# Gates and output product of the second layer multiplied as high and low parts, with high parts made by GpSimd

## The reference, cut to what matters

```
proj = h @ o_w_in                                   # h: 256 x 1024
(q_c, kc_, vc_, ks_, vs_, kw_, vw_, g_c, z_c, q_d, k_d, v_d, z_d) = split(proj)
o_c = nsa_attention(...)       # compressed, selected and window keys, 8 heads of 64
y_c = merge_heads(o_c) * silu(z_c)                  # 256 x 512
o_d = banded_attention(...)    # window 128, with sinks
y_d = merge_heads(o_d) * silu(z_d)                  # 256 x 512
y   = concatenate([y_c, y_d])                       # 256 x 1024
x   = x + y @ w_out[1]
```

## Time and profile before

| | |
|---|---|
| median of 3 runs | 909.28 us (907.03 to 910.65) |
| profiled execution | 910.96 us |
| its span | 909.2 us |
| mean granted clock of TensorE | 0.994 |
| busy: PE, PEld, DVE, ACT, POOL | 882.9, 826.0, 428.8, 446.7, 609.0 us |
| L656, GpSimd's subtractions, largest group | 328 times, mean 1313 ns |
| L1374, ScalarE's high parts | 82 times, mean 1914 ns |

### The profile page before, as it was taken

The page is one execution under the profiler, slowest core; times in us unless marked ns, Lnnn a source line. Parts: engine busy times, 40 slices in busy tenths (PEclk is TensorE's granted clock), DMA queues, the critical chain, the costliest instruction groups (busy, mean ns, idle before and its releaser), DMA issues.

```text
span 909.2 us, 16515 instructions
## 1 busy us (share of the span) xinstructions
PE 882.9 (97%) x6792; PEld 826.0 (91%) x6792; DVE 428.8 (47%) x952; ACT 446.7 (49%) x665; POOL 609.0 (67%) x485
## 2 busy tenths in 40 slices
PE   6999999899999999999999999999999999999997
PEld 5898889897777999888988799999999999999996
DVE  3998665743875466882445232331124562211001
ACT  3434667344555453354444547586334775533330
POOL 0766468740000669989777777768889999997880
PEclk9999999999999999999999999999999999999999
DMA  9844577783210279597666444444536655545421
GB/s 347 344 146 158 214 243 266 252 307 131 100 48 1 93 275 391 219 376 261 226 213 232 149 176 145 154 167 156 216 139 232 231 185 187 185 141 186 185 94 47
DMA packets 27907, 177.61 MB, mean 195 GB/s; under 512 B 3080, under 2 KB 5780, under 8 KB 7480
## 3 DMA queue, kind: packets, MB, share of 16 engines
q1 hardware_dynamic: 26248, 174.35, 53.1%
q10 hardware_dynamic: 1584, 2.20, 0.7%
HBM read 174.95 MB, written 3.43 MB: 196 GB/s over the span
## 4 chain that ended last, share of the span: by engine, by line
PE 90%; DVE 4%; ACT 2%; issue 1%; DMA 1%; POOL 1%; ACTq 0%; DVEq 0%; SPq 0%
PE proj L742 18%; PE proj L744 18%; PE proj L745 18%; PE proj L717 5%; PE proj L822 3%; PE proj L819 3%; PE proj L821 3%; PE proj L1016 3%; PE proj L778 2%; PE mixed L968 1%; PE proj L1089 1%; PE transposed L937 1%; PE scores L923 1%; PE mixed L951 1%; PE sums L876 1%
## 5 line engine op out<-in xcount | busy, mean ns | idle before, releaser
L656 POOL TENSOR_TENSOR w_lo<-raw,w_hi 128x512 fp32r<-128x512 f32 x328 | 418.9, 1313 | 208.2 <-ACT w_hi L1374 208.1
L744 PE MATMUL proj<-parts,w_lo 128*128 128x256 f32 x952 | 266.4, 280 | 0.6 <-POOL w_lo L656 0.6
L742 PE MATMUL proj<-parts,w_hi 128*128 128x256 f32 x904 | 257.3, 285 | 0.5 <-POOL w_lo L656 0.3
L745 PE MATMUL proj<-parts,w_hi 128*128 128x256 f32 x904 | 252.6, 279 | 0.0
L1374 ACT ACTIVATE w_hi<-raw 128x2048 fp32r<-128x2048 f32 x82 | 156.8, 1914 | 112.4 <-DMA raw<-in_weights 61.0
L744 PEld LDWEIGHTS proj<-parts,w_lo 128*128 128x128 f32 x952 | 179.1, 188 | 1.7 <-POOL w_lo L656 0.8
L742 PEld LDWEIGHTS proj<-parts,w_hi 128*128 128x128 f32 x904 | 169.9, 188 | 2.8 <-issue 2.1
L745 PEld LDWEIGHTS proj<-parts,w_hi 128*128 128x128 f32 x904 | 170.4, 188 | 0.0
L656 POOL TENSOR_TENSOR w_lo<-arena,w_hi 128x512 fp32r<-128x512 f32 (+2 forms) x44 | 56.2, 1317 | 56.5 <-ACT w_hi L1374 56.5
L742 PE MATMUL proj<-hid_hi,w_hi 128*128 128x256 f32 x160 | 45.3, 283 | 0.0
L819 PE MATMUL proj<-w_hi,parts 128*128 128x512 f32 x112 | 45.0, 402 | 0.0
(11 more groups left out here) (402 smaller groups left out, 2111.7 us busy)
## 6 DMA issues: line engine op xcount, KB each, us to landing
raw<-in_weights SPq DMA_DIRECT2D x105, 1024.0 KB, 5.0
arena<-in_weights SPq DMA_DIRECT2D x32, 1024.0 KB, 7.2
wide<-in_weights SPq DMA_DIRECT2D x9, 1024.0 KB, 7.0
probT<-in_weights SPq DMA_DIRECT2D x8, 1024.0 KB, 5.6
dil_lines<-dil_line SPq DMA_DIRECT2D x1, 2304.0 KB, 12.9
prob<-in_weights SPq DMA_DIRECT2D x2, 1024.0 KB, 4.9
dil_bias<-dil_lines SPq DMA_DIRECT2D x1, 1536.0 KB, 9.4
xT<-in_x SPq DMA_DIRECT2D x2, 512.0 KB, 5.8
```

The costliest lines, as they stand in the source:

```text
L656: nc.gpsimd.tensor_tensor(lo_slots[RAW_AT[n]][:, at], raw_slots[RAW_AT[n]][:, at], hi_slots[HI_AT[m]][:, at].bitcast(F32), ALU.subtract).t ...
L742: nc.tensor.matmul(dst, whi, h, start=first, stop=False)
L744: nc.tensor.matmul(dst, wlo, h, start=False, stop=False)
L745: last = nc.tensor.matmul(dst, whi, lo[:, k, :], start=False, stop=stop)
```

## The change

Seven units more are split: zc1, zd0, zd1, wo1_0 to wo1_3. For the last six (`PLACED`) GpSimd makes the high part itself, four copies of 128x512 (`high`), ahead of the four subtractions; ScalarE skips them in `passing`. The operand of the output product, y, is split in four pieces of two row blocks (`gathered_high` on ScalarE, `parts_low` on VectorE, new entries `L:y0`, `L:y1` of the table), and the first products of wo1_0 and wo1_1 are made side by side, on piece 0 in one round and on piece 1 in the next. The loads of ak2_0, ak2_1 and rq0 stand in the natural order, and from wo1_0 to ak2_1 a fourth slot for high parts is used, `w_hi_b`, over the space of `dil_bias`. The high parts of ak2_0, ak2_1 and rq0 are made at passing wo1_1, wo1_2 and wo1_3, one each.

```diff
 FILL_CD = [x.split() for x in (
-    "N:kd E:zc0", "zc1.0 E:kd", "zc1.1", "E:zc1", "modA zd0.0.0", "zd0.0.1 E:modA", "", "zd0.1", "zd1.0 E:zd0", "", "zd1.1.0",
-    "zd1.1.1", "", "H:wo1_0 E:zd1", "H:wo1_1", "")]
+    "N:kd E:zc0", "zc1.0 E:kd", "zc1.1", "E:zc1", "modA zd0.0.0", "zd0.0.1 E:modA", "",
+    "zd0.1", "zd1.0 E:zd0", "", "zd1.1.0", "zd1.1.1", "L:y0", "H:0 E:zd1 L:y1", "H:1", "")]
+PLACED = ("zd0", "zd1", *(f"wo1_{i}" for i in range(4)))
...
-SPLIT_SOON = ["bq1", "bk0", "bk1", "bv0", "bv1", "zb0", "zb1", "za0", "za1"] + [f"wo0_{i}" for i in range(4)] + ["kcvc", "kskw", "vsvw", "qc0", "qc1", "vdgt", "qd0", "qd1", "kd"]
+SPLIT_SOON = ["bq1", "bk0", "bk1", "bv0", "bv1", "zb0", "zb1", "za0", "za1"] + [f"wo0_{i}" for i in range(4)] + ["kcvc", "kskw", "vsvw", "qc0", "qc1", "vdgt", "qd0", "qd1", "kd", "zc1", *PLACED]
...
-    return EARLY if n >= WEIGHT_AT["wo1_0"] else [*range(NRAW), *EARLY]
+    return [*range(NRAW), *EARLY]
 
 
 RAW_AT, RAW_BEFORE = take_slots(WEIGHTS, raw_slots_of)
-HI_AT, HI_BEFORE = take_slots(SPLIT, lambda n, u: range(NHI + sum(n >= SPLIT_AT[start] for start in HI_MORE)))
+SHARED_HI = SPLIT[SPLIT_AT["wo1_0"]:SPLIT_AT["ak2_1"] + 1]
+HI_AT, HI_BEFORE = take_slots(SPLIT, lambda n, u: [*range(NHI), NHI + 1] if u in SHARED_HI else range(NHI + sum(n >= SPLIT_AT[start] for start in HI_MORE)))
...
-for _us, _before in ((BEFORE_NORM["x2"], "wo1_2"), (("rq0",), "wo1_3"), *(((u,), before) for u, before in zip(ADA_FIRST, FIRST_BEFORE)), *(((u,), before) for u, before in zip(ADA_LATE, LATE_BEFORE)),
+for _us, _before in (*(((u,), before) for u, before in zip(ADA_FIRST, FIRST_BEFORE)), *(((u,), before) for u, before in zip(ADA_LATE, LATE_BEFORE)),
...
+            def quarters(u):
+
+                kt, w = unit_shape(u)
+                return [slice(kt * w // 4 * i, kt * w // 4 * (i + 1)) for i in range(4)]
+
+            def high(u):
+
+                n, m = WEIGHT_AT[u], SPLIT_AT[u]
+                pool.wait_ge(proj_ready, GROUP_AT["zc0"] + 1 if u == SHARED_HI[0] else LAST_READ[SPLIT[HI_BEFORE[m]]] + 1)
+                pool.wait_ge(raw_in[RAW_AT[n]], raw_target(n))
+                for at in quarters(u):
+                    nc.gpsimd.tensor_copy(hi_slots[HI_AT[m]][:, at], raw_slots[RAW_AT[n]][:, at]).then_inc(sem("hi_pool"), 1)
+
             def low(u):
 
                 n, m = WEIGHT_AT[u], SPLIT_AT[u]
-                kt, w = unit_shape(u)
-                pool.wait_ge(hi_ready, m + 1)
-                for i in range(4):
-                    at = slice(kt * w // 4 * i, kt * w // 4 * (i + 1))
+                if u not in PLACED:
+                    pool.wait_ge(hi_ready, m + 1 - sum(SPLIT_AT[v] < m for v in PLACED))
+                for i, at in enumerate(quarters(u)):
+                    if u in PLACED:
+                        pool.wait_ge(sem("hi_pool"), 4 * PLACED.index(u) + i + 1)
                     nc.gpsimd.tensor_tensor(lo_slots[RAW_AT[n]][:, at], raw_slots[RAW_AT[n]][:, at],
                                             hi_slots[HI_AT[m]][:, at].bitcast(F32), ALU.subtract).then_inc(lo_ready, 1)
 
...
-                if u == "ak2_0":
+                if u == "zc1":
                     pool.wait_ge(proj_ready, GROUP_AT["hidv"] + 1)
                     nc.gpsimd.memset(probT[:, 0:512], 0.0).then_inc(sem("cmp_zero"), 1)
+                if u in PLACED:
+                    high(u)
                 low(u)
...
                 elif name[:2] == "H:":
-                    output_half(name[2:], 0, yT1, y_of)
+                    n = int(name[2:])
+                    state["pair"] = two_units(("wo1_0", "wo1_1"), gathered(n, n + 1), state["pair"] if n else None, done=False)
...
-            def output_half(name, half, y, piece):
-
-                plain(name, y, piece, range(KD // 2 * half, KD // 2 * (half + 1)), fresh=half == 0, done=half == 1)
+            def gathered(lo, hi):
+
+                return [((2 * n, 2 * n + 1), every, lambda k, n=n: pe.wait_ge(y_ready, 4 + n + 1)) for n in range(lo, hi)]
...
-                if i < 2:
-                    output_half(f"wo1_{i}", 1, yT1, y_of)
-                else:
-                    plain(f"wo1_{i}", yT1)
+                if i == 0:
+                    two_units(("wo1_0", "wo1_1"), gathered(2, 4), state["pair"])
+                elif i > 1:
+                    project(f"wo1_{i}")
...
-            def passing(name, most=len(SPLIT)):
-
...
+                    if v in PLACED:
+                        state["hi"] += 1
+                        continue
...
-                    nc.scalar.activation(dst, ready(name)[:], ACT.Tanh, scale=0.5).then_inc(sem("z_tanh"), 1)
+                    nc.scalar.activation(dst, ready(name, name not in PLACED)[:], ACT.Tanh, scale=0.5).then_inc(sem("z_tanh"), 1)
+                elif name[:3] == "L:y":
+                    gathered_high(int(name[3:]))
...
+            def gathered_high(n):
+
+                operand_high([(hi_of(n), two(yT1, n), [(proj_ready, GROUP_AT["zd1"] + 1), (po_free, STEPS_TO["b"] + 2 * n + 2)])])
...
             narrow_attention(PART["c"] + PART["d"], FILL_CD)
+            for n in (2, 3):
+                gathered_high(n)
             table(ACT.Sqrt)
             output_parts(1, "x2", gain1, 0)
...
+                elif name[:3] == "L:y":
+                    parts_low(yT1, [int(name[3:])])
...
-            narrow_attention(PART["c"] + PART["d"], FILL_CD, 1)
+            narrow_attention(PART["c"] + PART["d"], FILL_CD, 1, lambda: parts_low(yT1, [2]))
+            parts_low(yT1, [3])
```

More of the change, by code:

```diff
@@ L1171, in around_norm @@
                 gained_products(name, 1, range(KD))
-            y_of = lambda k: pe.wait_ge(po_free, STEPS_TO["b"] + 2 * (k // 2) + 2) if k % 2 == 0 else None
             def convolved_product(i):
@@ L1326, in _ @@
                 if name[1] == "r":
-                    wait = (lambda k: pe.wait_ge(y_ready, 4 + k // 2 + 1)) if i == 0 else None
+                    wait = (lambda k: pe.wait_ge(y_ready, 8 + k // 2 + 1)) if i == 0 else None
                     features(name, None, yret_lo, [[(f"{name}{x}", 0, 0)] for x in "ab"], wait)
@@ L1333, in merged_product @@
                 if i == 0:
-                    ready = lambda k: pe.wait_ge(y_ready, 12 + k // 2 + 1)
+                    ready = lambda k: pe.wait_ge(y_ready, 16 + k // 2 + 1)
                     two_units(("wo2_0", "wo2_1"), [(range(6), every, ready), (range(6, KD), every, ready)])
@@ L1356, in _, with passing @@
             state = dict(hi=0)
-            def passing(name, most=len(SPLIT)):
-                while state["hi"] < min(len(SPLIT), most):
+            def passing(name):
+                while state["hi"] < len(SPLIT):
                     m = state["hi"]
@@ L1368, in passing @@
                     kt, w = unit_shape(v)
-                    if HI_BEFORE[m] is not None:
-                        act.wait_ge(proj_ready, LAST_READ[SPLIT[HI_BEFORE[m]]] + 1)
-                    elif v in HI_MORE:
+                    if v in HI_MORE:
                         act.wait_ge(po_free, STEPS_TO["a"])
+                    elif old >= 0:
+                        act.wait_ge(proj_ready, old + 1)
                     act.wait_ge(raw_in[RAW_AT[n]], raw_target(n))
```

## The result

The changed kernel takes 917.9 us (median of 5 runs, 917.75 to 920.61) against 909.67 us (median of 5, 907.03 to 910.65): a ratio of 1.0108, 95% interval 1.009 to 1.0127, so it is slower by 8.2 us. Its profiled execution is one of 917.87 us with a span of 916.1, 6.9 us over both numbers of before.

A forecast was written before the change was run, and what follows sets the result against it. Bound: the VectorE–TensorE loop over the second layer's attention units, little slack on either. Terms −2.9 + 2.4 + 8.9 − 3.8 + 1.0 = +5.6 us on 910.96 gave 916.6, less 1.7 for the median: 914.9 us, range 905 to 921.

The forecast's parts named there:

- the step from profiled execution to median: Whole kernel: the median of the runs lies 1.7 us below the profiled execution, taking 916.6 to 914.9 us.
- shorter filling, what comes through: 64 split products inside the second layer's attention stage: −6.0 us in all, of which −2.9 us comes through.
- detour of y: Attention rounds: VectorE waits for ScalarE's high part of y's piece 0, making unit 13's transposes +2.4 us later.
- held time, with the clock: Attention stage: GpSimd's pieces hold VectorE's operations with two SBUF inputs, +8.9 us, plus lower TensorE clock, +1.0 us.
- end of the output product: 48 output products after the last mixing, split: 16.8 us for 20.64, −3.8 us.
- my walk: The sixteen attention rounds stepped through with the rows' durations: 16 holds, together 10.5 us, +8.9 us after slack.
- The clock: Attention stage: TensorE's clock falls after waits, 1.67 us for one fall; +1.0 us over before, bounds −1.7 and +6.7.
- The signs: Trace afterwards: L1943 at 1.9 to 2.3 us beside GpSimd, transposes of rounds 1 to 4 waiting 1 to 1.5 each.
- Only half of the hold: Attention stage: GpSimd's copies leave VectorE alone, only subtractions hold it; +2.2 us, 911.5 us; chance 0.28.
- Faster: Attention stage: holds fall in VectorE's slack or small operations slip between pieces; 903.3 to 905.0 us; chance 0.15.

The follow-up runs named there:

- no_gpsimd_y_behind: no_gpsimd_work with y's two subtractions inside the rounds put behind the normalising of units 13 and 14 on VectorE; 904.24 us.
- no_gpsimd_work: Changed kernel with GpSimd's copies and subtractions for the seven units cut to 128x2 copies, TensorE taking those weights from the operand's high part; 906.98 us.
- gates_only: Kernel before with only zc1, zd0 and zd1 split, GpSimd making the high parts of zd0 and zd1, output product plain; 910.23 us.
- half_pieces: Changed kernel with GpSimd's copies and subtractions of the six units cut into 128x256 pieces, twice as many of half the length; 925.89 us.
- y_one_round_later: Changed kernel with L:y0, L:y1 and the first products of wo1_0 and wo1_1 one round later; 920.17 us.
- y_later_with_gap: y_one_round_later with GpSimd's work on wo1_0 begun only after TensorE's sp_kd group, giving GpSimd a pause between two units; 917.87 us.
- output_only: Changed kernel with only wo1_0 to wo1_3 split, zc1, zd0, zd1 plain, high parts in the three usual slots; 924.83 us.
- late_units_early_loads: Kernel before with only wo1_2 and wo1_3 split, GpSimd starting on them after the last normalising, loads and slots rearranged so nothing is late; 907.54 us.

## Why the prediction was right

The direction and the mechanism were right, and the size nearly, in part by luck: +5.6 us forecast on the profiled execution, +6.9 measured (+8.2 between the medians, for my profile of before was 1.3 us above its median of five). The forecast of 914.9 was 3.0 us short of 917.9: 1.3 are the sum's, and 1.7 come from the step from profiled execution to median, which the changed kernel doesn't have (917.87 and 917.9).

| term | forecast | measured | from |
|---|---|---|---|
| shorter filling, what comes through | −2.9 | −1.5 | no_gpsimd_y_behind, stage 67.7 − 69.2 |
| detour of y | +2.4 | +1.7 | stage 69.4 − 67.7 |
| held time, with the clock | +8.9 + 1.0 | +9.8 | stage 79.2 − 69.4 |
| end of the output product | −3.8 | −3.5 | 17.1 − 20.6 |

The measured terms make +6.5 of the 6.9. They are differences taken one after another, on kernels without GpSimd's work first; in another order the overlaps would be shared out differently.

- *Held time.* 16 holds and 10.5 us were forecast, 16 holds and 9.07 us are in the trace. The copies are shorter than taken: 2.29/4 = 0.57 us for 0.7. That is also below the 0.77 us that the Trainium skill gives for 512 elements (page "GPSIMD Engine Reference", section 3.1, on elementwise cycle accounting), so here the measurement decides. By my walk shorter copies had to make the stage shorter than the +8.4 forecast; it came out at +10.0. The same page's rule of section 8, that GpSimd contends with VectorE where this has two SBUF inputs or runs in its 2-port mode, doesn't disagree with the trace: L1943 is held, and L1901, with an input in PSUM, isn't (1.11 us at 282.77 for four over 128x128, beside GpSimd). L1915, of one input, is held too; whether it ran in the 2-port mode the trace doesn't show.
- *The clock* was mis-sized. It was half in 227 to 233, 254 to 257 and 271 to 274. The last two falls follow waits on L1943 (1.09 us ahead of 253.37, 2.27 ahead of 269.74); the first began before the wait of 2.41 us, behind one of 0.90. Against the same work at the full clock it cost 0.45 (transposes at 230.50), 1.1 (the split products behind, 4.04 for 2.98), 1.67 (mixing at 253.96) and 1.0 (mixing at 270.8, 2.5 for 1.5), 4.2 us for 1.67 before: +2.5 or more where +1.0 stood. That and 9.1 of holds make 11.6, and 1.8 of it was under cover. As the two together are 9.8 us, some 7.3 are left for the holds where 8.9 stood. That the pair comes to 9.8 for a forecast 9.9 is luck: one was too large by about what the other was too small.
- *The filling* gave half of what I let through, and the detour 0.7 less than charged; these two errors cancel in part. In the changed kernel the wait of VectorE on ScalarE is short (0.68 us ahead of L2073), since VectorE was late anyway, but the subtraction stands in front all the same: L1928, whose exponentials were ready, starts 1.7 us after the end of L1920, with the normalising and TensorE's wait of 2.87 us behind it. So the detour shows at round 13, as the prediction asked.
- *The end* is as forecast, and GpSimd was nowhere late for TensorE from 200 to 400 us.
- *The signs.* L1943 at 2.26 and 1.23, TensorE's idle time and the end came as written. The transposes of rounds 1 to 4 were to wait 1 to 1.5 us each; they wait 2.41, nothing, 0.73 and 1.27. The last mixing ended 10.1 us later where 8 stood.
- *The rivals.* "Only half of the hold" would have needed copies that leave VectorE alone: L1920 at 281.26 took 0.49 us for 0.16 with only copies running on GpSimd (280.01 to 282.30). Its argument, that VectorE's operations with one input show no hold, was a misreading of the trace of before: a copy over 128x256, L2292 at 342.05, took 1.27 us beside GpSimd, where three others of that shape (L1820) took 0.41 each. "Faster" is what no_gpsimd_work shows, and only there. What I did not have at all is the long hold, though the trace of before has one. VectorE there (first the copy L2292), then GpSimd in the second place:

```profile
342.05 1.27 DVE L2292 COPY sq<-arena 128x256 f32<-128x256 f32 x1
...
672.15 4.02 DVE L2369 TENSOR_TENSOR arena<-arena 128x512 f32<-128x512 f32 x1
```

```profile
670.56 5.06 POOL L656 TENSOR_TENSOR w_lo<-raw,w_hi_a 128x512 fp32r<-128x512 f32 x4
```

The subtraction ends 0.55 us after the train, 3.3 us late; I had read only holds of one piece. The same subtraction is held 3.2 to 3.6 us in ten of the thirteen traces.

## What to carry to other kernels

Work given to an idle GpSimd can be paid by VectorE where VectorE's operations over SBUF lie on the path: here 11 us for 53 us more of GpSimd's time (662.0 − 609.0). Put it where VectorE has little of that kind to do, as at the end of the rounds, and look for holds through a whole train: in the one place tried here a pause between two trains cut such a hold. And an instruction that waits for a third engine goes behind the one that the critical engine wants, in its own list.

## What was not expected of the hardware

- A 0.16 us operation of VectorE was held 8.9 and 12.2 us, through 10 and 23 of GpSimd's pieces in a row, while others in like trains were let in after one. What decides is open. Four traces (gates_only, half_pieces, y_one_round_later, y_later_with_gap) have it at the same multiplication of the first unit, which lasts to the end of the train each time; in output_only it was let in after one piece with the train going on. So neither the instruction nor the train alone decides, and nothing was tried beyond the pause.
- Halving GpSimd's pieces halved the common hold (1.03 to 0.49 us), and the kernel was still 8 us slower, by the long hold ahead of the stage.
- The clock fell ahead of the stage in some traces and not in others: those of before and after have about 0.5 from 213 to 216 us, late_units_early_loads has no fall. From the sums of squares (L876, L894) to the first transposes it is 12.9 us (211.35 to 224.22) before and 11.2 (211.00 to 222.23) without the fall, with the same waits. It may be a part of why executions of the kernel before lie at 907 or at 909 to 911; none of the former was profiled.
